# Two layers of attention and routed experts: expert weights in a ring of three full sets, and routing by pairwise ranks

## The reference, cut to what matters

```python
for layer in range(DEPTH):                       # 2
    hx = modulate(rms_norm(x, norm_g[layer, 0]), mx[0], mx[1])     # hc the same for the context
    zx, zc = hx @ w_in[layer], hc @ w_in[layer]                    # 1024 -> 1952
    ox = latent_mix(...) @ w_out[layer]          # MLA, windowed, differential attention, pooling
    x = x + mx[2] * rms_norm(ox, norm_g[layer, 1])
    fx = hier_moe(modulate(rms_norm(x, norm_g[layer, 2]), mx[3], mx[4]), ...)
    x = x + mx[5] * rms_norm(fx, norm_g[layer, 3])

def hier_moe(h, ...):
    g_logits = tok @ gw + gb                     # 4 groups, the first of the largest is taken
    g_sel, p_g = argmax(g_logits), softmax(g_logits)[g_sel]
    e_in = (tok @ ew + eb)[group g_sel]          # 4 experts of that group
    top_v, top_i = lax.top_k(e_in, 2)
    w_sel = softmax(top_v) * p_g
    for e in range(16):
        gu = tok @ w_gu[e]                       # 1024 -> 2 x 512
        y += combine[:, e:e+1] * ((silu(gu[:, :512]) * gu[:, 512:]) @ w_down[e])
```

## Time and profile before

| | us |
|---|---|
| median of 3 runs (lowest, highest) | 1255.96 (1254.84, 1263.71) |
| the profiled execution | 1257.48 |
| its span | 1255.6 |
| TensorE busy | 995.3 (79% of the span) |
| VectorE, ScalarE, GpSimd busy | 312.8, 265.2, 162.4 |
| gate and up products (line 787), idle before them | 267.7, 142.3 |
| down products (line 800, from `W`) | 113.9 |
| moved by the DMA | 322.99 MB, mean 257 GB/s |

### The profile page before, as it was taken

How to read it: one execution, slowest core, us unless ns; L and a number is a source line. 1 busy time by engine, 2 the same in 40 slices (tenths; PEclk the granted TensorE clock), 3 DMA queues, 4 the chain that set the end, 5 groups by cost and what they waited for, 6 DMA issues and landing times. The chain is left out here.

```text
span 1255.6 us, 23117 instructions
## 1 busy us (share of the span) xinstructions
PE 995.3 (79%) x8828; PEld 609.9 (49%) x8829; DVE 312.8 (25%) x899; ACT 265.2 (21%) x702; POOL 162.4 (13%) x244
## 2 busy tenths in 40 slices
PE   4999999999996799769974389999997666655562
PEld 2354646655554566446752257756554443332241
DVE  1100064455435111101110500064424200000003
ACT  3111033445341011001100421044323000000001
POOL 0010024000022222112210200050002211110011
PEclk9899999999997799999998589999578787887786
DMA  9872547574366499999999512101018699999993
GB/s 378 300 252 86 205 186 279 213 293 146 108 249 255 139 383 388 410 411 391 363 411 407 211 34 101 67 2 35 1 46 344 265 410 409 410 410 410 410 358 114
DMA packets 99857, 322.99 MB, mean 257 GB/s; under 512 B 14346, under 2 KB 25524, under 8 KB 93524
## 3 DMA queue, kind: packets, MB, share of 16 engines
q1 hardware_dynamic: 70624, 279.19, 56.7%
q0 software_dynamic: 9216, 31.01, 7.1%
q10 hardware_dynamic: 19956, 11.95, 3.1%
HBM read 309.60 MB, written 18.81 MB: 262 GB/s over the span
## 5 line engine op out<-in xcount | busy, mean ns | idle before, releaser
L787 PE MATMUL psum<-weights,R 128*32 128x256 f32 x4032 | 267.7, 419 | 142.3 <-DMA weights<-in_exp_w_gu_dram 95.4
L787 PEld LDWEIGHTS psum<-weights,R 128*32 128x32 f32 x4032 | 159.8, 119 | 242.9 <-issue 194.3
L477 PE MATMUL psum<-hT,weights 128*128 128x512 f32 (+3 forms) x384 | 139.5, 524 | 4.6 <-DVE hT L1669 2.4
L1561 DVE STREAM_TRANSPOSE R<-R 128x256 f32<-128x256 f32 x66 | 29.4, 445 | 375.2 <-PE psum L787 364.7
L800 PE MATMUL psum<-weights,lat 128*32 128x256 f32 x1824 | 113.9, 388 | 3.5 <-issue 2.8
L477 PEld LDWEIGHTS psum<-hT,weights 128*128 128x128 f32 (+1 forms) x384 | 72.1, 190 | 69.7 <-issue 56.3
L1119 ACT ACTIVATE lat<-psum 128x128 f32<-128x128 f32 x64 | 17.8, 278 | 382.1 <-PE psum L787 379.3
L800 PEld LDWEIGHTS psum<-weights,lat 128*32 128x32 f32 x1824 | 73.2, 114 | 34.7 <-issue 7.8
L1333 DVE TENSOR_REDUCE st<-psum 128x1 f32<-128x512 f32 (+1 forms) x96 | 56.6, 599 | 102.5 <-PE psum L597 45.8
L1799 POOL DMA_INDIRECT R<-h_rows,slot_col x68 | 66.6, 980 | 54.2 <-POOL slot_col L1796 54.2
L618 PE MATMUL psum<-weights,R 128*128 128x64 f32 x480 | 68.4, 286 | 3.1 <-DVE rt_c L1387 1.1
(11 more groups left out here) (232 smaller groups left out, 952.1 us busy)
## 6 DMA issues: line engine op xcount, KB each, us to landing
weights<-in_exp_w_gu_dram SPq DMA_DIRECT2D x64, 2048.0 KB, 17.8
weights<-in_exp_w_down_dram SPq DMA_DIRECT2D x30, 2048.0 KB
weights<-in_ada_w_dram SPq DMA_DIRECT2D x24, 2048.0 KB, 7.5
weights<-in_w_in_dram SPq DMA_DIRECT2D x6, 2048.0 KB, 14.4
weights<-in_w_out_dram SPq DMA_DIRECT2D x4, 2048.0 KB, 7.9
y_rows<-lat ACTq DMA_DIRECT2D x252, 32.0 KB
y_rows<-in_constants_dram POOLq DMA_DIRECT2D x2, 3072.0 KB, 20.1
R<-vec_out POOLq DMA_DIRECT2D x9, 512.0 KB, 8.0
```

Of the source, the lines that this page charges most:

```text
L477: mm = nc.tensor.matmul(t[p0:p0 + m, lo:hi], w[:, k, col:col + m], hT[:, k, lo:hi], start=(k == 0), stop=(k == KD - 1))
L787: mm = nc.tensor.matmul(gu_ps[BLK * j:BLK * j + BLK, 0:256], xgT[:, k, :], w_gu[place][:, k, j, :, :, :], start=(k == 0), stop=(k == KD - ...
```

## The change

Three edits go together.

**A ring of three sets.** `hT` takes the `lo`, `R1` the `hi` and a new region `spare_w` the `dn` of a third set. `spare_w` also takes in small buffers that had their own space (`prob3`, `pab`, the squares, `rstd`, `ada_sb`, `w_rtb`, `row_src`). Experts go through places 0, 1, 2 in loops of three, the refill of e+3 waits for e. Queries, keys and values lie in `W[0]` in both layers, layer 1's projections are staged in `W[1]`, which expert 13 leaves, and all three are issued by expert 13's progress. `ya` and `yb` lie in `R1` and `spare_w`, the token rows and `xgT` in `lat`. The two `gate3` rows lie in `W[0]`, and POOL issues them when the last block has done its first half, before the gathers of expert outputs.

**Routing by ranks.** Each logit is compared with the four of its group at once; its rank is the number of larger ones plus equal ones before it. The group pick is rank 0, the chosen experts have rank below 2. A scan sums over tiles, so that TensorE needs three products. Counts are rounded up to 32 by an integer mask. The slot product is made four times, once per 32 partitions, from a one-hot table 32 wide. What the weights need (shifted group logits, their sum, the difference of the two best) is computed behind `slots`.

**Banks of the router constants.** VectorE's read of `rt_c` and ScalarE's copy of the row bank stand at the head of the mix step `rows_at(L) + 1`, before its maxima and its softmax; they stood in step `rows_at(L) + 2` and at the end of step `rows_at(L) + 1`.

```diff
+        spare_w = sb("spare_w", [P, 4 * D])
...
+        PIECES = ("lo", "hi", "dn")
+        pieces = [{name: part(W[i], n * 4 * D, 4 * D) for n, name in enumerate(PIECES)} for i in range(2)]
+        pieces.append({"lo": hT[:, :, :].rearrange("p k t -> p (k t)"), "hi": R1[:, :], "dn": spare_w[:, :]})
+        w_gu = [[w[name].rearrange("p (k c b j r) -> p k j c b r", k=4, c=2, b=4, j=QUADS) for name in PIECES[0:2]] for w in pieces]
+        w_dn = [w["dn"].rearrange("p (k n) -> p k n", k=4) for w in pieces]
...
-            places[name] = [part(W[L % 2], o, n, s, **kw) for L in range(DEPTH)]
+            places[name] = [part(W[0], o, n, s, **kw) for L in range(DEPTH)]
...
-        gate3_row = [part(R1, (2 + s) * D, D) for s in range(2)]
-        ya = [part(W[1], 2 * i * D, D) for i in range(4)]
-        yb = [part(W[1], (2 * i + 1) * D, D) for i in range(4)]
+        gate3_row = [part(W[0], s * D, D) for s in range(2)]
+        ya = [part(R1 if i < 2 else spare_w, i % 2 * 2 * D, D) for i in range(4)]
+        yb = [part(R1 if i < 2 else spare_w, (i % 2 * 2 + 1) * D, D) for i in range(4)]
...
-        buffers += [n % 3 for n in range(len(items) - n_stage0)]
+        buffers += [3 + n % 3 for n in range(len(items) - n_stage0)]
...
+                nc.tensor.matmul(t[:, 0:n], C("before"), chosen[:, 0:n], start=True, stop=False)
+                nc.tensor.matmul(t[:, 0:n], ones[:, :], prefix[:, 0:n], start=False, stop=True)
+                nc.tensor.matmul(t[:, n:n + 16], ones[:, :], prefix[:, 0:n].rearrange("p (e t) -> p e t", t=nt)[:, :, nt - 1], start=True, stop=True)\
+                    .then_inc(*mark(S, ("filled", "rk", L)))
                 pe.wait_ge(*at("slot_hot", L))
                 t = take("st", L)
                 for i in range(2 * nt):
-                    mm = nc.tensor.matmul(t[:, 0:COLS], place_hot[:, i, :], block_id[:, i, :],
-                                          start=(i == 0), stop=(i == 2 * nt - 1))
+                    for a in range(QUADS):
+                        mm = nc.tensor.matmul(t[BLK * a:BLK * a + BLK, 0:COLS], place_hot[:, i, :], block_id[:, i, :],
+                                              start=(i == 0), stop=(i == 2 * nt - 1), skip_group_check=True)
                 mm.then_inc(*mark(S, ("filled", "st", L)))
...
+                for place in range(3):
+                    expert(0, place, first=(place == 0))
+                with pe.Fori(1, N_EXP // 3) as triple:
+                    for place in range(3):
+                        expert(triple, place)
+                expert(N_EXP // 3, 0)
                 total = pe.value_load(tabs[L][0:1, T_TOTAL:T_TOTAL + 1], min_val=N_EXP, max_val=MAXBLK)
-                down(total - 1, odd)
+                down(total - 1, 0)
...
+                    if i == rows_at(L) + 1:
+                        copy(S, row_sb[0:64, :], ("rowT", L), P, hi=64, keys=[("row_sb", L)])
...
+                        t = read(v, "rt_c", L)[:, 0:40].rearrange("p (s c) -> p s c", s=2)
+                        v.wait_ge(*at("rows", L))
+                        tt_(rt_c[:, :, :], t, rt_b[:, L, :].unsqueeze(1).to_broadcast([P, 2, 20]), ALU.add)\
+                            .then_inc(*mark(S, ("read", "rt_c", L)))
...
+                ne, m = 16 * nt, 5 * nt
+                v.wait_ge(*at("read", "lg", L, nt - 1))
+                x4 = lg[:, 0:4 * m].rearrange("p (m j) -> p m j", j=4)
+                other, own = x4.unsqueeze(2).to_broadcast([P, m, 4, 4]), x4.unsqueeze(3).to_broadcast([P, m, 4, 4])
+                over4, tied4 = (x[:, 0:16 * m].rearrange("p (m j i) -> p m j i", j=4, i=4) for x in (over, tied))
+                tt_(tied4, other, own, ALU.is_equal).then_inc(*mark(S, ("tied", L)))
+                tt_(over4, other, own, ALU.is_gt).then_inc(*mark(S, ("over", L)))
+                v.wait_ge(*at("tied", L))
+                tied16 = tied[:, 0:16 * m].rearrange("p (m c) -> p m c", c=16)
+                tt_(tied16, tied16, C("earlier").unsqueeze(1).to_broadcast([P, m, 16]), ALU.mult).then_inc(*mark(S, ("tied_earlier", L)))
+                v.wait_ge(*at("tied_earlier", L))
+                step(tt_(over[:, 0:16 * m], over[:, 0:16 * m], tied[:, 0:16 * m], ALU.add))
+                step(red(rank[:, 0:4 * m], over[:, 0:16 * m].rearrange("p (m i) -> p m i", i=4), AX.X, ALU.add))
+                ts(at_most[:, 0:ne], rank[:, 4 * nt:20 * nt], 2.0, None, ALU.is_lt)
+                step(ts(gpick[:, 0:4 * nt].rearrange("p (g t) -> p t g", t=nt), rank[:, 0:4 * nt].rearrange("p (t g) -> p t g", t=nt), 0.0, None, ALU.is_equal))
+                step(tt_(chosen[:, 0:ne].rearrange("p (g j t) -> p g t j", g=4, t=nt), at_most[:, 0:ne].rearrange("p (g t j) -> p g t j", g=4, t=nt),
+                         gpick[:, 0:4 * nt].rearrange("p (g t) -> p g t", t=nt).unsqueeze(3).to_broadcast([P, 4, nt, 4]), ALU.mult))
+                step(nc.vector.tensor_tensor_scan(prefix[:, 0:ne], C(f"within{L}"), chosen[:, 0:ne], 0.0, ALU.mult, ALU.add),
+                     ("chosen", L))
...
+                t = read(v, "rk", L)
+                step(ts(cnt_i[:, 0, :], t[:, ne:ne + 16], float(BLK - 1), None, ALU.add))
+                step(ts(cnt_i[:, 1, :], cnt_i[:, 0, :], -BLK, None, ALU.bitwise_and))
+                step(ts(nb32[:, 1:17], cnt_i[:, 1, :], float(BLK), None, ALU.max))
+                step(nc.vector.tensor_tensor_scan(start32[:, :], ones[:, 0:17], nb32[:, :], 0.0, ALU.mult, ALU.add))
+                place = vals[:, 0, 0:ne].rearrange("p (t e) -> p t e", t=nt)
+                step(tt_(place, t[:, 0:ne].rearrange("p (e t) -> p t e", t=nt), start32[:, 0:16].unsqueeze(1).to_broadcast([P, nt, 16]), ALU.add), ("read", "rk", L))
+                step(tt_(pos_of[:, :, 0:ne], picked[:, :, 0:ne], vals[:, 0, 0:ne].unsqueeze(1).to_broadcast([P, 2, ne]), ALU.mult))
+                step(red(rs[:, 11:13, 0:nt], pos_of[:, :, 0:ne].rearrange("p w (t e) -> p w t e", t=nt), AX.X, ALU.add))
+                step(nc.vector.tensor_copy(spos[:, 0:2 * nt].rearrange("p (w t) -> p w t", w=2), rs[:, 11:13, 0:nt]), ("spos", L))
...
+                tt_(place_hot[:, 0:n2, :], spos_f[:, 0, 0:n2].unsqueeze(2).to_broadcast([P, n2, BLK]),
+                    C("count")[:, 0:BLK].unsqueeze(1).to_broadcast([P, n2, BLK]), ALU.is_equal).then_inc(*mark(S, ("place_hot", L)))
+                tt_(block_id[:, 0:n2, :], spos_f[:, 1, 0:n2].unsqueeze(2).to_broadcast([P, n2, COLS]),
+                    C("count")[:, 0:COLS].unsqueeze(1).to_broadcast([P, n2, COLS]), ALU.is_equal).then_inc(*mark(S, ("block_id", L)))
+                v.wait_ge(*at("place_hot", L))
+                tt_(place_hot[:, 0:n2, :], place_hot[:, 0:n2, :], C(f"token{L}").unsqueeze(2).to_broadcast([P, n2, BLK]), ALU.mult)\
+                    .then_inc(*mark(S, ("slot_hot", L)))
...
-                for s in range(nt // 2):
-                    vector_row(L, ROW_GATE3, s, gate3_row[s], "gate3_row")
...
+                g_.wait_ge(sem(f"lo_done{L}"), total)
+                g_.sem_inc(sem("hold"), 1)
+                for s in range(tiles(L) // 2):
+                    vector_row(L, ROW_GATE3, s, gate3_row[s], "gate3_row")
...
-                    cum = sp.value_load(tabs[L - 1][0:1, T_CUM + N_EXP - 2:T_CUM + N_EXP - 1], min_val=1, max_val=MAXBLK)
-                    for n, done in enumerate(("lo_done", "gu_done")):
+                    cum = sp.value_load(tabs[L - 1][0:1, T_CUM + N_EXP - 3:T_CUM + N_EXP - 2], min_val=1, max_val=MAXBLK)
+                    for n, done in enumerate(DONE.values()):
                         sp.wait_ge(sem(f"{done}{L - 1}"), cum)
                         sp.sem_inc(sem("sp_hold"), 1)
                         load(lo + n)
-                    lo += 2
-                    sp.wait_ge(*at("yb", L - 1, q_tokens(L - 1) // P - 1))
+                    lo += 3
...
                     load_piece(L, 1, 1, piece)
                 sp.wait_ge(*at("filled", "lg", L, tiles(L) - 1))
-                dn = A["exp_w_down"][L, 2].rearrange("(k p) n -> p k n", p=P)
-                for k in range(4):
-                    sp.dma_start(w_dn_ahead[k], dn[:, k, :]).then_inc(*mark(f"dma_ahead{L}", *([("ahead", L)] if k == 3 else []), by=16))
+                load_piece(L, 2, 2, "lo")
+                for tt in range(tiles(L)):
+                    sp.wait_ge(*at("h_stored", L, tt))
+                load_piece(L, 2, 2, "hi")
+                load_piece(L, 2, 2, "dn")
                 sp.wait_ge(*at("tab", L))
...
+                def next_expert(triple, place):
+                    cum = sp.value_load(tabs[L][0:1, ds(triple * 3 + (T_CUM - 3 + place), 1)], min_val=1, max_val=MAXBLK)
+                    for piece, done in DONE.items():
+                        load_piece(L, triple * 3 + place, place, piece)
+                with sp.Fori(1, N_EXP // 3) as triple:
+                    for place in range(3):
+                        next_expert(triple, place)
+                next_expert(N_EXP // 3, 0)
```

227 lines of the change are left out of this document (81 added, 146 removed).

## The result

The changed kernel is faster, by much more than forecast. In five rounds of alternation its median is 1209.31 us (six executions) against 1257.05 us (17 of before); the ratio is 0.9622 with a 95% interval of 0.9595 to 0.9649. The forecast was 1230 and the range ended at 1216.

A forecast was written before the change was run, and what follows sets the result against it. The expert phases were taken as bound by the weight DMA queue near 410 GB/s, 5.12 us per piece. Terms -14.8, +2.5, -10.5 and -2.8 sum to -25.6 us: 1257.5 to 1231.9, at the median 1230 us, range 1216 to 1243.

The forecast's parts named there:

- The mix: Both layers' mixes: router constants' banks read one step earlier, ending TensorE's waits: -2.8 us, bounds 0 and -3.5.
- Layer 0's expert phase: Fewer remaining pieces -10.2, queue shortfall -7, later block 1 +2.4: -14.8 us in all.
- The two pieces and the shortfall: Layer 0's expert phase: 39 pieces remain instead of 41, -10.2 us; slices below 410 GB/s filled, -7 of 8.8 us.
- Rival 1: Layer 0: small loads drain beside the backlog without holding ScalarE, phase starts 5 us earlier: 1223 us; chance 0.14.
- The handoff: Layer 0 to layer 1: added projection and gate3 loads delay the gathers of expert outputs: +2.5 us, bounds 0 and +7.7.
- rival 2: Handoff to layer 1 costs in full, gathers finishing behind all the added loads: 1235 us; chance 0.12.
- Layer 1's expert phase: Two more early pieces fill idle DMA time, gate3 row moves to the end: -10.5 us, bounds 0 and -14.
- Routing: Slot list ready 5 us earlier in layer 0, 4 in layer 1; neither credited to the end.
- Rival 4: Expert phases: token gathers become the bound, at 14 us landing a block takes 8 us: 1289 us; chance 0.03.
- Rivals 3: Third set hardly works as a ring: layer 0's shortfall stays, layer 1's first refill 5 us late: 1242 us; chance 0.08.
- 5: As a rival: the mix's reads buy nothing and routing's new shapes are slow: 1235 us; chance 0.05.
- The start: Stretch from the start to expert 0's issue in layer 0: -1.1 us.

The follow-up runs named there:

- 9: The changed kernel with layer 1's 16 narrow products issued at the end of its mix: 1208.35 to 1214.29 us in all six, ratio 0.9636 to before.
- 10: The kernel before with only layer 1's narrow products, and the read of their result, moved to the end of its mix: 1229.80 us median, ratio 0.9802.
- experiment 8: The changed kernel with layer 1's small weights loaded early by SyncE, not by ScalarE behind the routing: 1201.87 us median, ratio 0.9563 to before.
- experiment 3: The kernel before with the new routing alone: ratio 0.9962 to before, -4.8 us.
- 4: The kernel before with the mix's edit alone: four executions from 1227.27 to 1232.72 us (ratio 0.9780), three from 1254.24 to 1256.83.
- 1: The changed kernel again, no edit: ratio 0.9622 to before; five executions from 1207.63 to 1211.29 us, one of 1240.96.
- 6: The changed kernel with the mix's edit in layer 1 only: 1208.86 to 1215.39 us in three of six (ratio 0.9643), 1236.61 to 1242.67 in the others.
- 12: The changed kernel with small weights issued early by SyncE and layer 1's narrow products at its mix's end: 1200.88 us median, ratio 0.9566 to before.
- run 11: The kernel before with 24 dense products that nothing reads added in step 18 of layer 1's mix: 1248.00 us median of ten, ratio 0.9941.
- 2: The kernel before with the ring of three sets alone: ratio 0.9871 to before, -16 us.

## Why the prediction was wrong, by its own steps

- **The mix: wrong, and this is the step that failed.** "TensorE waited for them 1.08 us in layer 0, 0.29 + 1.45 us in layer 1, and is the path there: -2.8 us; bounds 0 (the next reader of a bank is just as late) and -3.5." The waits went as said. But the 1.45 us were charged at their own length, and behind them came 48 us at half clock: in layer 1's mix -25.5 us where 1.7 stood. Both were in the trace of before: the page's clock slices show a 5 in slice 29, with TensorE at 9 beside it. I had read the clock as a property of the kernel that no edit moves.
- **Without the clock the sum was nearly right**, by three readings of which none is clean. All stretches but layer 1's mix sum to -22.5 us in the quicker profile, for -23.9 forecast. Kernel 5, with everything but layer 1's part of the mix's edit, is at 0.9811 of before, -23.7 us; with the wait of 1.45 and the 0.29 beside it that is -25.5, against -25.6 forecast; but its profiled execution has 58 us of half clock and before's 48. Kernels 9 and 10 are both free of the stretch and differ by the rest of the change: 1229.80 to 1210.26, -19.5 us (-20.8 by the ratios), where the forecast less the wait of 1.45 is -24.2.
- **Layer 0's expert phase**: -14.8 forecast, -12.7 measured (quicker profile), -10.1 in the slower. Block 1 starts 2.1 us later against expert 0's issue (86.15 us before, 88.24 now), forecast +2.4. The two pieces and the shortfall, -17.2 together, gave -14.8 from there to the last product (257.94 to 243.12 us). The slices are full, so I put the rest down to the tail, where TensorE's last product starts 28.3 us behind the issue of the last piece instead of 19.0; no run tries that.
- **Rival 1**, that the small loads needn't hold ScalarE, was worth 7.4 us in the forecast's arithmetic and 7.4 (layer 0's phase -7.3) when an edit made it true. That the two agree is luck: block 1 came 5.2 us earlier, not 7.4, and the rest was the clock (experiment 8). As a forecast of the change it was wrong: they did hold ScalarE, to 420.52.
- **The handoff**: +2.5 forecast, +2.65 measured; rival 2 (+7.5) fell.
- **Layer 1's expert phase**: -10.5 forecast, -11.7 measured. Ring and routing give -7.5 and -1.3 alone, so about 3 us exist only together. As forecast, the routing gain keeps the first refill from being late behind the longer backlog: with the ring alone it is issued 60.1 us behind expert 0's issue and the queue moves 102 and 261 GB/s in the ten us around it; in the quicker profile it comes at 57.6 us, and the queue moves 401 and 385.
- **Routing** was credited to neither phase; alone it gives -4.8 us.
- **Rival 4** fell: the row gathers land in 2.9, 5.9 and 6.6 us (least, median, most) in the quicker profile, not slower than before. Rivals 3 and 5 fell with the slices and with experiments 3 and 4.
- **The start**: the slower profile's first 340 us are 5.1 us shorter than before's, of which some 4 are an early dip of the clock (0.85 in before's 20:40, 1.00 there) and no work of the change (the profile of experiment 3, with before's ring and mix, has 1.00 there too).

What stays open: why the narrow products bring the clock down in one execution and not in the next. With them, and without the wait, 15 of 24 executions of runs 1, 4 and 6 and the first runs of the changed kernel came through; without both, 18 of 18 (9, 10 and 12). Six of these are kernel 12's, which shares 8's edit; the twelve of 9 and 10 would come through by chance in 0.4% of cases at 15 in 24. And kernel 8 has the narrow products and came through five times of five, as it would one time in ten at 15 in 24, so its mix may simply stand better. What part of the small work fails to lift the clock, the transposes or the products of 64 rows or columns, wasn't tried.

## What to carry to other kernels

Read the granted clock beside TensorE's busy share before pricing a wait. Where windows show TensorE busy throughout at 0.50, find the row where the clock fell and the row where it rose: a small wait there can cost half of the whole distance between them (24 to 29 us here), and the edit to price is the removal of the dip, or some dense work moved behind it. And time both kernels often enough to see whether one has two modes, and profile one of each.

## What the runs showed of the hardware

- TensorE, busy without a gap, stayed at half its clock for 48, 58 and 82 us in layer 1's mix; each time it rose during the pooling products or up to 1.1 us behind them, and in run 11 1.1 us into 24 added products of 128x128 by 128x256.
- In layer 0's mix, where groups of 16 products of 128x512 stand among the small ones, the clock fell behind the wait of 1.08 us in four of six profiles and was back in 3 to 4 us.
- A wait of 0.84 us was followed by the fall in five of six executions; of the kernels with 1.45 us of wait in layer 1's mix, and the narrow products ahead of it (before, 2, 3 and 5), none of 66 executions came through.
- The added products of run 11 took 0.23 us per recorded pass of 256 columns, the first 1.1 of their 11.13 us at half clock; the same scores group takes 1.98 us at 1.00 and 3.78 at 0.50.
